# Depthwise convolution: 16 of 31 taps on TensorE as four passes over four stacked, shifted copies of 32 channels, the copies made through memory, and no taps on GpSimd

## The chip, the cores and the metric

The kernel runs on one core of one Trainium2 chip, as one launch. The metric is the device time of that launch in microseconds; of several runs the median counts.

## The reference

Two decoder layers over 256 tokens of width 1024, all in float32. Layer 0 mixes tokens with a causal Conformer convolution, layer 1 with sparse attention; behind each stand a mixture of 32 experts and a gated per-layer embedding. Only the convolution module of layer 0 is touched:

```python
def conv_module(xn, w_pw1, b_pw1, w_dw, b_dw, ln_g, ln_b, w_pw2, b_pw2):
    u = xn @ w_pw1 + b_pw1
    a, g = jnp.split(u, 2, axis=-1)
    u = a * jax.nn.sigmoid(g)
    u = lax.conv_general_dilated(          # depthwise, 31 taps, causal
        u, w_dw[:, None, :].astype(u.dtype), window_strides=(1,),
        padding=[(CONV_WIDTH - 1, 0)], dimension_numbers=("NWC", "WIO", "NWC"),
        feature_group_count=u.shape[-1]) + b_dw
    u = jax.nn.silu(layer_norm(u, ln_g, ln_b))
    return u @ w_pw2 + b_pw2
```

## The kernel before

Each engine has a program of its own, written out by hand, and the programs meet at semaphores. The 1024 channels of the convolution are eight chunks `c` of 128 channels; channels lie on the partitions and the 256 tokens along the free dimension. For one chunk the work goes round the engines:

- TensorE makes both halves of the first pointwise product (L494, `pw1(c)`, 16 matmuls that the trace counts as 32) and signals `pw1_mm`.
- ScalarE takes the sigmoid of the gate half (L1051, `sig_ok`), and then scales the identity by six tap weights into six diagonal matrices (L1057, `dg_ok`).
- VectorE multiplies both halves into the padded row `cv0[:, c]` (L1287, the function `glu`, `glu_ok`). It does this for chunk c+1 only when its own taps of chunk c are through.
- The 31 taps of the chunk are then shared out. VectorE does 20 of them, one instruction each, in two running sums (L1302, L1304, L1306). GpSimd does 5, nine instructions (L955, L958, L959, `ptap_ok`). TensorE does the last 6 as matmuls with the diagonal matrices (L473, the function `taps`, `tap_mm`).
- VectorE adds up the four partial sums (L1316 to L1318, `conv_ok`), and TensorE adds the chunk into the channel sum for the layer norm (L479, `channel_sum`).

TensorE's order is `pw1(c)`, `taps(c-1)`, `channel_sum(c-3)`. From chunk 4 on `pw1(c)` also waits for `glu(c-3)`, since the products share four PSUM banks. Behind the last chunk TensorE does `taps(7)`, the four bias products of the second pointwise layer (L504), the channel sums that are left, and signals `lnmm`; VectorE then starts the layer norm (L1321). The second pointwise product (L518), the router and the 32 experts follow in one chain.

All loads of weights are issued by the SP queue in a fixed order: the four parts of the first pointwise weights (L350), the second (L352), expert 0 (L307, L311). `ple_w_gate` (L357, 4 MB) waits for `pw1(3)`; one block of attention weights (L359) and a third of expert 1 (L307), 4 MB together, wait for `pw1(7)`. The experts' weights go through two slots of a ring (`ring`), and a slot is loaded again when its expert is done. ScalarE issues a few small loads at the very start (L1031) and none later.

Of the kernel before, what the change touches and what calls it, by code (L numbers as in the profile page):

```python
# [65 lines left out]
def build(nc, x, p, positions, g_mix, g_ffn, g_ple, conv_w_pw1, conv_b_pw1, conv_w_dw, conv_b_dw,  # L66
# [3 lines left out]
    with ExitStack() as ctx:  # L70
# [125 lines left out]
        accb = [carve(256) for _ in range(2)]  # L196
        dgb = carve(2 * PE_TAPS * P).rearrange("p (b i q) -> p b i q", b=2, i=PE_TAPS)
        pac = [ppw[:, 2304:2560], ppw[:, 2560:2816]]
        ptm = ppw[:, 2816:3072]
# [661 lines left out]
        def _(pool):  # L861
# [84 lines left out]

            for c in range(KD):
                pool.wait_ge(glu_ok, c + 1)
                if c >= 2:
                    pool.wait_ge(conv_ok, c - 1)  # L950
                for i_ in range(POOL_TAPS):
                    w = TAPS - PE_TAPS - POOL_TAPS + i_
                    u = cv0[:, c, w:w + T]
                    if i_ == 0:
                        g.tensor_scalar(pac[c % 2], u, wdw[:, c, w:w + 1], None, ALU.mult).then_inc(c_pool, 1)  # L955
                        own[0] += 1
                    else:
                        link(g.tensor_scalar(ptm, u, wdw[:, c, w:w + 1], None, ALU.mult))  # L958
                        i = g.tensor_tensor(pac[c % 2], pac[c % 2], ptm, ALU.add)  # L959
                        if i_ < POOL_TAPS - 1:  # L960
                            link(i)
                i.then_inc(ptap_ok, 1)
                pool.wait_ge(ptap_ok, c + 1)
# [748 lines left out]
```

## Time and profile before

| | |
|---|---|
| time, median of 3 runs | 1471.85 us (1470.04 to 1474.88) |
| time of the profiled execution | 1465.78 us |
| span of the profiled execution | 1464.1 us |
| busy: TensorE matmul, VectorE, ScalarE, GpSimd | 1094.6, 344.3, 250.8, 476.2 us |
| moved by DMA | 448.75 MB, 307 GB/s on average |

Busy time is summed over the whole span, whose stages have different limits; the convolution takes the first tenth of it. In the rows of the trace the first number of a timeline is the start in us from the beginning of the span, the second the time taken; PE is TensorE's matmul, PEld its weight load, DVE VectorE, ACT ScalarE, POOL GpSimd, and SPq and ACTq are the times that the queues of SP and ScalarE need to issue a DMA.

### The profile page before, as it was taken

To read this page: it belongs to the slowest core of one execution; us is meant where nothing else is said; L and a number is where in the kernel's file an instruction comes from. 1 tells how busy PE (TensorE), PEld (TensorE's weight loads), DVE (VectorE), ACT (ScalarE), POOL (GpSimd) and SP (SyncE) were. 2 spreads that over 40 slices of the span, in tenths; PEclk is the share of its full clock that TensorE was granted. 3 is DMA by queue.
4 is the path that set the end of the run, shared out by engine and by line. 5 is a ranking of instruction groups with operands and counts; after the bars stand their busy time and mean duration, and the time that the engine had idled before them with its cause. 6 is when DMAs were issued, how large, how long until landed. Compare 5 with 4: busy or idle time off the path is not lost.

```text
span 1464.1 us, 27412 instructions
## 1 busy us (share of the span) xinstructions
PE 1094.6 (75%) x10298; PEld 631.2 (43%) x10299; DVE 344.3 (24%) x958; ACT 250.8 (17%) x598; POOL 476.2 (33%) x799
## 2 busy tenths in 40 slices
PE   5976986766767667677999789876767677677658
PEld 5863553333433333333455554533433334334334
DVE  3997140000000000002417681400000000000011
ACT  3112111110111101111211571111101101011111
POOL 3662043334343343431000130434343343434320
PEclk9996998888888878888999699988888878889879
DMA  8921229999999999998313603599999999998940
GB/s 260 397 103 64 115 74 407 414 413 415 413 414 413 413 415 413 415 413 308 121 56 126 278 2 115 194 414 415 413 415 413 414 414 413 415 412 330 414 179 29
DMA packets 119819, 448.75 MB, mean 307 GB/s; under 512 B 10562, under 2 KB 21442, under 8 KB 103394
## 3 DMA queue, kind: packets, MB, share of 16 engines
q1 hardware_dynamic: 115202, 447.91, 77.0%
q10 hardware_dynamic: 4576, 0.30, 0.2%
q8 instruction: 26, 0.43, 0.1%
q14 instruction: 15, 0.12, 0.0%
HBM read 447.14 MB, written 1.05 MB: 306 GB/s over the span
## 4 chain that ended last, share of the span: by engine, by line
PE 37%; DMA 35%; DVE 6%; issue 4%; PEldq 3%; ACT 2%; PEld 1%; POOL 1%; SPq 1%; POOLq 0%; DVEq 0%
DMA ring<-in_moe_w_up 35%; PE PS L542 13%; PE PS L430 9%; PE PS L557 5%; PE PS L518 2%; PEld PS L564 1%; PEldq L642 1%; PE PS L550 1%; DVE arena L1353 1%; SPq L307 1%; PE PS L729 1%; PE PS L702 1%; ACT arena L1099 1%; PEldq L643 1%; ACT arena L1095 1%
## 5 line engine op out<-in xcount | busy, mean ns | idle before, releaser
L542 PE MATMUL PS<-ring,arena 128*32 128x256 f32 x4128 | 356.2, 516 | 233.9 <-DMA ring<-in_moe_w_up 222.3
L542 PEld LDWEIGHTS PS<-ring,arena 128*32 128x32 f32 x4128 | 170.5, 147 | 410.4 <-issue 252.9
L920 POOL TENSOR_SCALAR arena<-arena 128x32 f32<-128x32 f32 x64 | 18.8, 293 | 538.8 <-PE PS L564 538.8
L1353 DVE TENSOR_TENSOR arena<-PS,arena 64x256 f32<-64x256 f32 x65 | 27.8, 428 | 671.1 <-ACT arena L1095 666.5
L557 PE MATMUL PS<-ring,arena 128*32 128x256 f32 x2080 | 126.0, 381 | 30.8 <-DVE arena L1356 30.8
L1095 ACT ACTIVATE arena<-PS 64x256 f32<-64x256 f32 x64 | 24.2, 378 | 594.7 <-PE PS L542 594.7
L902 POOL TENSOR_SCALAR arena<-arena 128x512 f32<-128x512 f32 x67 | 104.7, 1562 | 3.5 <-DVE arena L1405 3.5
L557 PEld LDWEIGHTS PS<-ring,arena 128*32 128x32 f32 x2080 | 73.4, 109 | 61.1 <-issue 37.5
L895 POOL TENSOR_SCALAR arena<-arena 128x32 f32<-128x32 f32 x268 | 92.5, 366 | 13.6 <-POOL arena L921 13.2
L904 POOL TENSOR_TENSOR arena<-arena 128x512 f32<-128x512 f32 x67 | 85.2, 1272 | 5.6
L564 PE MATMUL PS<-arena 32*128 32x256 f32 x1040 | 74.5, 397 | 9.4 <-ACT arena L1112 0.6
L529 PE MATMUL PS<-hn,arena 128*32 128x256 f32 x1072 | 70.4, 379 | 3.0 <-POOL arena L898 2.1
L430 PE MATMUL PS<-wb,xnT 128*128 128x512 f32 x160 | 71.9, 606 | 0.0
L1348 DVE TENSOR_TENSOR arena<-PS,g 128x256 f32<-128x256 f32 x67 | 28.5, 425 | 170.0 <-PE PS L535 170.0
L889 POOL TENSOR_TENSOR rstd<-rstd,nhalf 128x1 f32<-128x1 f32 x12 | 8.2, 696 | 158.4 <-DVE rstd L1250 158.4
L564 PEld LDWEIGHTS PS<-arena 32*128 32x128 f32 x1040 | 50.3, 183 | 20.2 <-issue 20.2
L1099 ACT COPY arena<-PS 128x256 f32<-128x256 f32 x64 | 23.9, 373 | 168.5 <-PE PS L557 168.5
L906 POOL TENSOR_TENSOR arena<-arena 128x256 f32<-128x256 f32 x67 | 48.8, 728 | 5.3
L1095 ACT ACT_TABLE_LOAD x32 | 41.1, 1283 | 41.2 <-issue 41.1
L430 PEld LDWEIGHTS PS<-wb,xnT 128*128 128x128 f32 x160 | 30.8, 196 | 37.7 <-issue 37.7
L529 PEld LDWEIGHTS PS<-hn,arena 128*32 128x32 f32 x1072 | 33.6, 110 | 27.7 <-POOL arena L898 3.1
L1306 DVE SCALAR_TENSOR_TENSOR arena<-ppw,arena 128x256 f32<-128x256 f32 x72 | 45.1, 626 | 0.0
(309 smaller groups left out, 1271.0 us busy)
## 6 DMA issues: line engine op xcount, KB each, us to landing
ring<-in_moe_w_up SPq DMA_DIRECT2D x64, 2048.0 KB, 17.5
ring<-in_moe_w_down SPq DMA_DIRECT2D x64, 2048.0 KB, 22.1
ring<-in_moe_w_gate SPq DMA_DIRECT2D x63, 2048.0 KB, 12.9
wb<-in_ple_w_gate SPq DMA_DIRECT2D x4, 2048.0 KB, 20.6
ring<-in_conv_w_pw SPq DMA_DIRECT2D x3, 2048.0 KB, 19.3
ring<-in_nsa_w_in SPq DMA_DIRECT2D x3, 2048.0 KB, 18.2
wb<-in_nsa_w_in SPq DMA_DIRECT2D x2, 2048.0 KB, 9.0
wb<-in_nsa_cmp_w SPq DMA_DIRECT2D x2, 2048.0 KB, 8.4
```

The lines of the kernel that those rows point to most:

```text
L430: i = pe.matmul(PS[:, bank, :], lhs[:, k, t * P:(t + 1) * P], w[:, k, :], start=start and k == 0, stop=(k == KD - 1))
L529: i = pe.matmul(PS[32 * j:32 * j + 32, BGX, 0:Q4], lhs[:, t, :], hn[:, t, Q4 * j:Q4 * (j + 1)], start=(t == 0), stop=(t == NT - 1))
L542: i = pe.matmul(PS[32 * j:32 * j + 32, BGU, 0:256], xT[:, k, :], w[:, k, 256 * (j % 2):256 * (j % 2 + 1)], start=(k == 0), stop=(k == 7))
L557: i = pe.matmul(PS[32 * j:32 * j + 32, BY, 0:Q4], hT[:, c, 32 * f:32 * f + 32], w_dn(s)[:, f, c, Q4 * j:Q4 * (j + 1)], start=(q == 0), sto ...
L564: i = pe.matmul(PS[:, ACC + j, 256 * t:256 * (t + 1)], w[32 * j:32 * j + 32, t * P:(t + 1) * P], ysb[32 * j:32 * j + 32, :], start=False, ...
L895: i = g.tensor_scalar(eq4[:, t, k, :], c32, S4[:, t, k:k + 1], None, ALU.is_equal)
L902: g.tensor_scalar(eqr, srow, cc, None, ALU.is_equal).then_inc(count, 1)
L904: g.tensor_tensor(eqr, eqr, wrow, ALU.mult).then_inc(count, 1)
L906: g.tensor_tensor(to_wT, eqr[:, 0, :], eqr[:, 1, :], ALU.add).then_inc(w_ok, 1)
L1095: nc.scalar.activation(gs[64:128, :], PS[0:64, BGU, 0:256], ACT.Silu).then_inc(sil_ok, 1)
L1306: i = v.scalar_tensor_tensor(out=o, in0=u, scalar=wdw[:, c, w:w + 1], in1=o, op0=ALU.mult, op1=ALU.add)
L1353: return v.tensor_tensor(hh[64:128, :], PS[64:128, BGU, 0:256], gs[64:128, :], ALU.mult)
```

## The change

TensorE does 16 taps in place of 6, GpSimd none in place of 5, and VectorE 15 in place of 20. To put 16 taps into few matmuls, the 128 rows of the array are used as four taps of 32 channels each: an operand `xst` holds, for a group `q` of 32 channels, four copies of the row, each shifted by one token more, one on each quarter of the partitions. Sixteen matmuls of 128 rows and 32 columns (four passes `m` for each of four groups `q`) then do 16 taps of 128 channels. Their weights `dgb` are built by GpSimd in one instruction a chunk, from a 0/1 pattern `stk` and the tap weights `wst`.

[...] ScalarE's queue writes the row of the chunk to memory (`xdram`, 128 rows of 1084 bytes), waits until it is there, and reads it back in four DMAs, one for each shift (each 32 partitions x 4 groups, pieces of 1072 bytes). The tap weights take the same way once, ahead of the first sigmoid, in rows of 512 bytes and pieces of 128 bytes. Line numbers of the changed kernel are 9 higher from SP's program on, 10 in GpSimd's.

```diff
-PE_TAPS, POOL_TAPS = 6, 5
+PE_TAPS, STACK = 16, 4
+RUNS = PE_TAPS // STACK
+DVE_TAPS = TAPS - PE_TAPS
+XW = T + STACK * (RUNS - 1)
...
             def taps(c):
-                pe.wait_ge(glu_ok, c + 1)
                 pe.wait_ge(dg_ok, c + 1)
                 if c >= 2:
                     pe.wait_ge(conv_ok, c - 1)
-                for i_ in range(PE_TAPS):
-                    w = TAPS - PE_TAPS + i_
-                    i = pe.matmul(PS[:, 4 + c % 2, 0:T], dgb[:, c % 2, i_, :], cv0[:, c, w:w + T],
-                                  start=(i_ == 0), stop=(i_ == PE_TAPS - 1))
+                pe.wait_ge(xst_in[c % 2], 16 * STACK * (c // 2 + 1))
+                for m in range(RUNS):
+                    for q in range(4):
+                        i = pe.matmul(PS[32 * q:32 * q + 32, 4 + c % 2, 0:T], dgb[c % 2][:, q, m, :],
+                                      xst[c % 2][:, q, STACK * m:STACK * m + T], start=(m == 0), stop=(m == RUNS - 1))
                 i.then_inc(tap_mm, 1)
...
+            link(g.tensor_scalar(stk[:, :], iot[:, :], colp[:, 0:1], None, ALU.is_equal))
+            pool.wait_ge(wst_in, 16 * (1 + STACK))
             for c in range(KD):
-                pool.wait_ge(glu_ok, c + 1)
                 if c >= 2:
-                    pool.wait_ge(conv_ok, c - 1)
-                for i_ in range(POOL_TAPS):
...
+                    pool.wait_ge(tap_mm, c - 1)
+                shape = [P, 4, RUNS, 32]
+                g.tensor_tensor(dgb[c % 2], stk[:, :].unsqueeze(1).unsqueeze(1).broadcast_to(shape),
+                                wst[:, :, c, :].unsqueeze(3).broadcast_to(shape), ALU.mult).then_inc(dg_ok, 1)
...
             norm(0, ROW_MIX)
+            act.wait_ge(vec_ok, 4)
+            act.dma_start(wdram, wch.rearrange("p j c m -> p (j c m)")).then_inc(wst_in, 16)
+            act.wait_ge(wst_in, 16)
+            for j in range(STACK):
+                act.dma_start(wst[32 * j:32 * j + 32, :, :, :].rearrange("p q c m -> p q (c m)"),
+                              wdram.rearrange("(q p) (j n) -> j p q n", q=4, j=STACK)[j]).then_inc(wst_in, 16)
             for c in range(KD):
...
                 if c >= 2:
                     act.wait_ge(tap_mm, c - 1)
-                for i_ in range(PE_TAPS):
-                    w = TAPS - PE_TAPS + i_
-                    i = nc.scalar.activation(dgb[:, c % 2, i_, :], ident[:, :], ACT.Copy, scale=wdw[:, c, w:w + 1])
-                i.then_inc(dg_ok, 1)
+                act.wait_ge(glu_ok, c + 1)
+                act.dma_start(xdram[c], cv0[:, c, DVE_TAPS:]).then_inc(xst_out, 16)
+                act.wait_ge(xst_out, 16 * (c + 1))
+                for j in range(STACK):
+                    act.dma_start(xst[c % 2][32 * j:32 * j + 32, :, :],
+                                  xdram[c].rearrange("(q c) u -> c q u", q=4)[:, :, j:j + XW]).then_inc(xst_in[c % 2], 16)
...
-                nv = TAPS - PE_TAPS - POOL_TAPS
-                for w in range(nv):
-                    o = cT[:, c, :] if w % 2 == 0 else accb[0]
+                for w in range(DVE_TAPS):
+                    o = cT[:, c, :] if w % 2 == 0 else accb
...
                 dve.wait_ge(c_dve, own[0])
+                link(v.tensor_tensor(cT[:, c, :], cT[:, c, :], accb, ALU.add))
                 dve.wait_ge(tap_mm, c + 1)
-                dve.wait_ge(ptap_ok, c + 1)
-                link(v.tensor_tensor(accb[1], PS[:, 4 + c % 2, 0:T], pac[c % 2], ALU.add))
-                link(v.tensor_tensor(cT[:, c, :], cT[:, c, :], accb[0], ALU.add))
-                v.tensor_tensor(cT[:, c, :], cT[:, c, :], accb[1], ALU.add).then_inc(conv_ok, 1)
+                v.tensor_tensor(cT[:, c, :], PS[:, 4 + c % 2, 0:T], cT[:, c, :], ALU.add).then_inc(conv_ok, 1)
```

How this stands in ScalarE's program, from the copies of the normed input (L1017) over chunks 0 and 1 to chunk 2, before the change:

```order
L1017 ACTIVATE xnT<-PS,vecT 128x128 x3
L1051 ACT_TABLE_LOAD
L1051 ACTIVATE arena<-PS,vecT 128x256 [waits pw1_mm]
L1057 ACTIVATE arena<-ident,arena 128x128 x6
L1051 ACTIVATE arena<-PS,vecT 128x256 [waits pw1_mm]
```

and in the changed kernel, the same place, as far as the sigmoid of chunk 1 (`tap_rows` and `glu_rows` are the tensors in memory):

```order
L1018 ACTIVATE xnT<-PS,vecT 128x128 x3
L1049 DMA tap_rows<-arena 128x128 [waits vec_ok]
L1052 DMA arena<-tap_rows 32x4x32 [waits wst_in]
L1052 DMA arena<-tap_rows 32x4x32 x3
L1058 ACT_TABLE_LOAD
L1058 ACTIVATE arena<-PS,vecT 128x256 [waits pw1_mm]
L1063 DMA glu_rows<-ppw 128x271 [waits glu_ok]
L1066 DMA ppw<-glu_rows 32x4x268 [waits xst_out]
L1066 DMA ppw<-glu_rows 32x4x268 x3
L1058 ACTIVATE arena<-PS,vecT 128x256 [waits pw1_mm]
```

The six scalings have gone, and five DMAs a chunk have come, with a wait between the first and the others; the next sigmoid stands behind them in the same queue.

TensorE's program at the end of the convolution, from the last pointwise product to the layer norm's second sum, before the change:

```order
L494 MATMUL PS<-xnT,ring 128x256 [waits xt_act] x4
L473 MATMUL PS<-ppw,arena 128x256 [waits conv_ok,dg_ok,glu_ok]
L473 MATMUL PS<-ppw,arena 128x256 x5
L479 MATMUL PS<-hn,ones 128x256 [waits conv_ok]
L473 MATMUL PS<-ppw,arena 128x256 [waits conv_ok,dg_ok,glu_ok]
L473 MATMUL PS<-ppw,arena 128x256 x5
L504 MATMUL PS<-arena,ones 128x512 x4
L479 MATMUL PS<-hn,ones 128x256 [waits conv_ok] x3
L509 MATMUL PS<-xnT,ones 128x256 [waits ln_sq] x8
```

and in the changed kernel:

```order
L503 MATMUL PS<-xnT,ring 128x256 [waits xt_act] x4
L482 MATMUL PS<-ppw 32x256 [waits xst_in0,conv_ok,dg_ok]
L482 MATMUL PS<-ppw 32x256 x15
L488 MATMUL PS<-hn,ones 128x256 [waits conv_ok]
L482 MATMUL PS<-arena 32x256 [waits xst_in1,conv_ok,dg_ok]
L482 MATMUL PS<-arena 32x256 x15
L513 MATMUL PS<-arena,ones 128x512 x4
L488 MATMUL PS<-hn,ones 128x256 [waits conv_ok] x3
L518 MATMUL PS<-xnT,ones 128x256 [waits ln_sq] x8
```

The order of the pieces is the same; the taps are 16 matmuls in place of 6, and their wait is now for the copies (`xst_in`) and no longer for the row itself (`glu_ok`).

## Rows read from the trace of the kernel before

**Rows 1.** The page: DMA share in 40 slices of the span, and the chain's shares.

```profile
DMA  8921229999999999998313603599999999998940
PE 37%; DMA 35%; DVE 6%; issue 4%; PEldq 3%; ACT 2%; PEld 1%; POOL 1%; SPq 1%; POOLq 0%; DVEq 0%
```

**Rows 2.** Timeline of chunk 6, VectorE and TensorE; brackets: idle before, releaser.

```profile
89.43 0.47 DVE L1287 SCALAR_TENSOR_TENSOR ppw<-PS,vecT,arena 128x256 f32<-128x256 f32 x1
...
99.11 0.47 DVE L1306 SCALAR_TENSOR_TENSOR arena<-ppw,arena 128x256 f32<-128x256 f32 x1
99.51 0.47 DVE L1306 SCALAR_TENSOR_TENSOR hn<-ppw,arena,hn 128x256 f32<-128x256 f32 x1
...
101.89 0.47 DVE L1287 SCALAR_TENSOR_TENSOR ppw<-PS,vecT,arena 128x256 f32<-128x256 f32 x1
...
102.41 4.54 PE L473 MATMUL PS<-ppw,arena 128*128 128x256 f32 x12 [2.26 <-DVE ppw L1287]
```

**Rows 3.** Timeline of the first chunks, TensorE, ScalarE and VectorE.

```profile
27.97 0.47 ACT L1051 ACTIVATE arena<-PS,vecT 128x256 f32<-128x256 f32 x1 [5.29 <-PE PS L494]
...
34.68 2.75 PE L473 MATMUL PS<-ppw,arena 128*128 128x256 f32 x12
...
37.27 7.07 PE L494 MATMUL PS<-xnT,wb 128*128 128x256 f32 x32
...
56.27 0.59 PE L479 MATMUL PS<-hn,ones 128*128 128x256 f32 x2
```

**Rows 4.** Timeline of the end of the convolution, TensorE and VectorE.

```profile
114.86 5.49 PE L473 MATMUL PS<-ppw,arena 128*128 128x256 f32 x12 [7.47 <-DVE ppw L1287]
120.28 3.82 PE L504 MATMUL PS<-arena,ones 1*128 1x512 f32 x8
124.02 2.08 PE L479 MATMUL PS<-hn,ones 128*128 128x256 f32 x4
...
127.87 0.42 DVE L1318 TENSOR_TENSOR hn<-hn,arena 128x256 f32<-128x256 f32 x1
129.68 0.42 DVE L1321 TENSOR_SCALAR arena<-PS 128x256 f32<-128x256 f32 x1 [1.38 <-PE PS L479]
```

**Rows 5.** The chain that ended last, one piece of the experts' stage.

```profile
206.23 1.97 PE PS L557 x32
```

**Rows 6.** The page's groups: a two-input GpSimd instruction of 512 elements.

```profile
L904 POOL TENSOR_TENSOR arena<-arena 128x512 f32<-128x512 f32 x67 | 85.2, 1272 | 5.6
```

**Rows 7.** DMA issues: count, KB each, median us to landing.

```profile
ring<-in_conv_w_pw SPq DMA_DIRECT2D x3, 2048.0 KB, 19.3
...
ppw<-in_p SPq DMA_DIRECT2D x1, 256.0 KB, 2.7
...
out_h<-h SPq DMA_DIRECT2D x1, 512.0 KB, 2.6
```

**Rows 8.** SP's DMA queue from 34 to 36 and 50 to 54 us: packets, MB, share.

```profile
q1 hardware_dynamic: 370, 0.76, 101.8%
...
q1 hardware_dynamic: 410, 1.64, 102.6%
```

**Rows 9.** Timeline: issues of DMAs by SP and ScalarE.

```profile
7.13 1.79 ACTq L1031 DMA_DIRECT2D posi<-in_positions  x1
...
25.34 9.96 SPq L352 DMA_DIRECT2D ring<-in_conv_w_pw  x2
...
43.66 2.66 SPq L311 DMA_DIRECT2D ring<-in_moe_w_down  x1
...
53.87 7.14 SPq L357 DMA_DIRECT2D wb<-in_ple_w_gate  x2
...
100.60 0.58 SPq L307 DMA_DIRECT2D ring<-in_moe_w_gate  x1
```

**Rows 10.** Stretches of two us: length, busy by engine, granted clock, DMA.

```profile
104.00:106.00 2.00, 2.00 (x6) 1.56 (x5) 2.00 (x4) 0.00 (x0) 1.82 (x3) 0.50 1.05 406
...
118.00:120.00 2.00, 2.00 (x6) 1.35 (x4) 2.00 (x5) 0.00 (x0) 1.82 (x3) 0.50 0.00 0
```

More of the change, by code:

```diff
@@ L77, in build @@
         PS = ctx.enter_context(nc.psum_tensor("PS", [P, 8, 512], F32))
+        xdram = nc.dram_tensor("glu_rows", (KD, P, T + STACK * RUNS - 1), F32, kind="Internal").ap()
+        wdram = nc.dram_tensor("tap_rows", (P, STACK * 8 * RUNS), F32, kind="Internal").ap()
         ring = sb("ring", [P, 2, 12288])
@@ L98, in build @@
         colp = sb("colp", [P, 1])
+        stk = sb("stk", [P, 32])
         xtot = sb("xtot", [P, 1])
@@ L195, in build @@
         wdw = carve(8 * TAPS).rearrange("p (c w) -> p c w", c=8)
[L196 to L199, printed above, removed]
+        accb = carve(256)
+        wch = carve(STACK * 8 * RUNS).rearrange("p (j c m) -> p j c m", j=STACK, c=8)
+        wst = carve(8 * 4 * RUNS).rearrange("p (q c m) -> p q c m", q=4, c=8)
+        xst = [x_.rearrange("p (q u) -> p q u", q=4) for x_ in (ppw[:, 2304:2304 + 4 * XW], carve(4 * XW))]
+        dgb = [x_.rearrange("p (q m s) -> p q m s", q=4, m=RUNS) for x_ in (ppw[:, 3392:3392 + 512], carve(512))]
         bpw2 = carve(1024)[0:1, :]
@@ L252, in build @@
         att_in, gate_in, mask_ok, c_bld = sem("att_in"), sem("gate_in"), sem("mask_ok"), sem("c_bld")
-        tap_mm, dg_ok, ptap_ok, root_in, root_ok = sem("tap_mm"), sem("dg_ok"), sem("ptap_ok"), sem("root_in"), sem("root_ok")
+        tap_mm, dg_ok, wst_in, root_in, root_ok = sem("tap_mm"), sem("dg_ok"), sem("wst_in"), sem("root_in"), sem("root_ok")
+        xst_in, xst_out = [sem(f"xst_in{i}") for i in range(2)], sem("xst_out")
         x_bld = sem("x_bld")
@@ L884, in _ @@
                 link(g.iota(ioti[32 * q:32 * q + 32, 0:1], pattern=[[0, 1]], base=0, channel_multiplier=1))
-            g.tensor_copy(colp[:, :], ioti[:, 0:1]).then_inc(const_ok, 1)
+            link(g.tensor_copy(colp[:, :], ioti[:, 0:1]))
+            g.memset(mcol[:, 6:7], 0.0).then_inc(const_ok, 1)
             def rsqrt(n, x):
@@ L945, in _ @@
             rsqrt(2, rstd[:, 1, 1:2])
+            link(g.tensor_scalar(stk[:, :], iot[:, :], colp[:, 0:1], None, ALU.is_equal))
+            pool.wait_ge(wst_in, 16 * (1 + STACK))
             for c in range(KD):
-                pool.wait_ge(glu_ok, c + 1)
                 if c >= 2:
-                    pool.wait_ge(conv_ok, c - 1)
-                for i_ in range(POOL_TAPS):
[L952 to L963, printed above, removed]
+                    pool.wait_ge(tap_mm, c - 1)
+                shape = [P, 4, RUNS, 32]
+                g.tensor_tensor(dgb[c % 2], stk[:, :].unsqueeze(1).unsqueeze(1).broadcast_to(shape),
+                                wst[:, :, c, :].unsqueeze(3).broadcast_to(shape), ALU.mult).then_inc(dg_ok, 1)
             rsqrt(3, rstd[:, 1, 0:1])
@@ L1276, in first_columns @@
                 dve.wait_ge(vtr, 3)
-                v.tensor_copy(wdw, PS[:, 2, 0:8 * TAPS].rearrange("p (c w) -> p c w", c=8)).then_inc(vec_ok, 1)
-                dve.wait_ge(vec_ok, 3)
+                taps = PS[:, 2, 0:8 * TAPS].rearrange("p (c w) -> p c w", c=8)
+                v.tensor_copy(wdw, taps).then_inc(vec_ok, 1)
+                v.tensor_copy(wch, taps[:, :, DVE_TAPS:].rearrange("p c (m j) -> p j c m", j=STACK)).then_inc(vec_ok, 1)
+                dve.wait_ge(vec_ok, 4)
                 link(v.memset(cv0[:, :, 0:TAPS - 1], 0.0))
```

## The prediction

> **What bounds the kernel now.** I read the page first: its chain of waits gives TensorE 37% and DMA 35%, and the DMA share over the span shows where, at 9 in the two experts' stages and 1 or 2 in the third to the sixth slice [rows 1]. The change lies in the first 130 us, so the question is whether the end of the convolution passes on to the end of the kernel. It does: the experts' weights are loaded when a slot of the ring comes free, so that stage starts as late as its first expert, and nothing with a time of its own stands between. I therefore count the moment at which VectorE starts the layer norm, 129.7 us [rows 4], and carry its shift to the end one for one.
>
> Within the convolution I read the timeline. One chunk takes 101.89 - 89.43 = 12.5 us, and VectorE has no gap in it: it is the bound [rows 2]. Its taps run 0.40 us apart where GpSimd is silent [rows 2]; 20 of them with the product for the next chunk (0.4) and three additions (1.4) make 9.8 us, and the other 2.7 are what GpSimd's taps cost VectorE. TensorE needs 7.1 us for the pointwise product, 2.75 for six taps, 0.6 for a sum, 10.4 in all, and waits 2 us or more in each late chunk [rows 2, 3]. Behind the last chunk TensorE's taps, the bias products and two sums are done by 126.1, before VectorE's last addition at 127.9 to 128.3; after that only one sum is left, 1.4 us to the layer norm [rows 4].
>
> **What the change takes away.** VectorE: 15 taps (6.1 us), the product (0.4) and two additions (0.9) are 7.4 us a chunk. GpSimd's one instruction of 512 elements takes 1.3 [rows 6] and can hold VectorE up by no more than that: 8.7 at worst. ScalarE's six scalings are off. TensorE: 16 matmuls of 32 columns are 32 instructions in the trace's count, and 32 such took 1.97 us in the experts [rows 5], less than the 2.75 of now. So TensorE becomes the bound at 7.1 + 2.0 + 0.6 = 9.7 us a chunk, unless the copies are late.
>
> **What the bounce costs with a quiet DMA.** The trace has no such bounce; the nearest rows bound it. A write of 512 KB to memory lands 2.6 us after issue, a read of 256 KB 2.7 us [rows 7]. At the 0.4 MB/us that the engines move [rows 8], the write of 139 KB is 0.9 shorter: 1.8. Four reads of 137 KB leave about 0.4 us apart, so the last lands 1.3 + 2.7 = 4.0 after the first issue. Together 5.8 us from the gated row to the copies, below the 9.7 of a chunk: quiet, it is hidden in all chunks but the last. The Trainium skill (SBUF — State Buffer, "The DMA setup-cost knee") speaks against the change here: about 2 us fixed per transfer whatever its size, which by an estimate from its fit is 2.3 for the write where the row gives 1.8. By the page the three exposed bounces would cost 1.5 us more than in the sum below.
>
> **What it costs with a busy DMA.** From the start to about 75 us SP's loads keep all engines full [rows 1, 8]. Pieces of 2 KB took 370 in 2 us x 16 engines, 88 ns each; pieces of 4 KB 410 in 4 us, 160 ns [rows 8]. The write gives each engine 8 pieces, the reads 32. If ScalarE's pieces and SP's alternate, the write gains 0.7 and the reads 2.8 us beside 2 KB pieces (9.3 in all), 1.3 and 5.1 beside 4 KB (12.2). Lower bound nothing (5.8), if a small queue is served at once.
>
> A second cost is the issue. SP's own queue is held 5 us for one DMA of 2 MB (9.96 for two, 7.14 for two later), and ScalarE once 1.8 us for a load of 0.5 KB while SP was also issuing [rows 9]. If the descriptors of both queues come from one place, a DMA of ScalarE can stand up to 5 us behind one of SP's, twice in a bounce: between 0 and 10 us. I take 1.3 a side, half of the mean of that wait, for chunks 0, 1 and 3, which fall beside SP's held issues (until 46 us, and when `ple_w_gate` is issued behind `pw1(3)`) [rows 9]. When SP issues behind `pw1(7)` it is not held (0.58 us) [rows 9]; there I take 1 in all.
>
> **The sum**, as times of the new kernel:
> - `pw1(1)` ends at 34.7, as now [rows 3]. The tap weights' own bounce stands ahead of the first sigmoid, which starts at 27.97 now after 5.3 us of idle. Those 5.3 us hide a quiet bounce up to its last issue; beside SP's loads I take 1.5 us more than they hide (0 to 4), so the row of chunk 0 is gated at 30.5.
> - Chunk 0: 5.8 + 3.5 + 2.6 = 11.9, copies at 42.4. TensorE, which now starts its taps at 34.7, waits 7.7 us. Two chunks of taps and product (9.1 each) bring `pw1(3)` to 60.6; chunk 1's copies (ScalarE is through with chunk 0's reads at 37.3, VectorE with its taps at 36.6; gated at 38.2, there at 50.1) are in time.
> - Chunk 2: product ready at 51.5, gated 1.1 later, 12.2 beside 4 KB pieces: 64.8. TensorE waits 4.2 us.
> - Four chunks of 9.7 end `pw1(7)` at 103.6. Chunk 3 (11.9) is in time; chunk 4, still beside SP's backlog since ScalarE adds 0.69 MB a chunk, is 0.7 late: 104.3. Now it ends at about 100, where SP's next DMAs leave [rows 9].
> - Chunk 7: gated at 105.4. SP has just issued 4 MB behind the same product, 2 KB and then 4 KB pieces: 5.8 + 0.7 + 4.0 + 1.0 = 11.5, copies at 116.9.
> - What is queued behind those copies on TensorE now stands in the path: taps (2.0 at full clock; 3.9, which I take, at half after such a wait), bias products 3.8, three sums (0.6 each, 1.0 at the lower clock) 2.2 [rows 3, 4]. The layer norm can start at 126.8, against 129.7: 2.9 us gained.
> - The clock. After its idle 2.3 us the 12 tap instructions at 102.4 took 4.5 us and after 7.5 us 5.5, not 2.75, with a granted clock of 0.50, the 1.2 GHz level, in the stretches there [rows 2, 4, 10]. The waits of 7.7 and 4.2 us can each bring that: 0 to 5.4 us in all, of which I take 1.8, what the short wait cost.
>
> Left is a gain of 1.1 us. The profiled execution of now, 1465.78 in all, would be one of about 1464.7; it lies 6.1 below the median of the runs, so for the median 1471.85 - 1.1 = 1470.7 us. In short: VectorE's 40 us (8 x 5) are saved, and TensorE, the bounces and the tail eat them.
>
> **The rivals.** A measurement of this kernel tells about 0.3%, 4.4 us, from no change.
> - *Forecast: it cancels out, within 4.4 us of now.* Chance 0.36; its own range 1467 to 1476.
> - *Faster: ScalarE's DMAs are served past SP's.* For it: its loads at the start were issued in 0.4 to 1.8 us with SP's queue full. With 5.8 us for chunks 0 to 6 TensorE never waits after chunk 0; chunk 0 is there at 36, `pw1(7)` ends at 93, and with 10.5 for chunk 7 and 10 for the tail the layer norm starts at 114: 15.5 gained, 1456. With the pieces alternating but no held issue it is 5 to 6 us, 1466. Chance 0.33 for both. Against it: the queue was full and a load took 19.3 us to land [rows 7].
> - *Slower: ScalarE's DMAs stand behind SP's in issue.* Place: chunks 0, 1 and 3 while SP is held. Each us more a side costs about 2 us for chunk 0 and, when chunk 1 or 3 is late too, 1 to 2 more. At 4 us a side chunk 0's copies come at 50, chunk 3's 5 late, and `pw1(7)` ends past 115: 12 us lost, 1484. It decides from about 2.5 us a side on, where the loss passes 4.4. Chance 0.27.
> - *Slower by another way: VectorE stays the bound.* From its cycle of 8.7 at worst against 9.7 I give this 0.04.
>
> **The numbers.** Faster by over 0.3%: 0.33; within: 0.36; slower: 0.31. The range leaves out the best of the fast case and the worst of the slow one: 1457 to 1484.
>
> **What would show it.** In the changed kernel's trace: VectorE's taps 0.40 apart, and gaps in VectorE that were not there. Taps on TensorE of 2 us at full clock. Idle of TensorE before the taps of chunks 0, 2 and 7, released by the read DMAs: 8, 4 and 10 us; none before 1, 5 and 6. ScalarE's issues: write to first read 1.8 us late in the stage, over 3 early. `pw1(7)` at 104, the layer norm 10 us behind the last copies. I am wrong if reads issued before 60 us land within 5 us (faster), or if ScalarE's queue is held for several us at one issue (slower); or if the shift at the layer norm is not the shift at the end.

## The result, and the profile after

The changed kernel takes 1487.22 us (median of 4 runs, 1480.12 to 1490.93) against 1471.4 (4 runs): ratio 1.0098, 95% interval 1.0056 to 1.0141. It is slower, and the forecast of no measurable change (1470.7, range 1457 to 1484) was wrong. The profiled execution takes 1480.12 us with a span of 1478.4, 14.3 more than before; the layer norm starts at 145.16, 15.5 later than in [rows 4]. So the shift does pass on to the end, and what is lost is lost in the convolution.

The page of the changed kernel: DMA share in 40 slices, and the chain's shares by engine and by line; the copies and the write (`glu_rows`) are in it with 2% each.

```profile
DMA  8955028999999999999303801589999999999950
PE 41%; DMA 40%; DVE 6%; issue 4%; ACT 3%; PEldq 2%; PEld 1%; SPq 1%; POOL 1%; ACTq 0%; POOLq 0%; DVEq 0%
DMA ring<-in_moe_w_up 35%; PE PS L551 13%; PE PS L439 9%; PE PS L566 5%; PE PS L527 2%; DMA arena<-glu_rows 2%; PE PS L503 2%; DMA glu_rows<-ppw 2%; PEld PS L573 1%; PEldq L651 1%; PE PS L559 1%; DVE arena L1361 1%; SPq L316 1%; PE PS L738 1%; PE PS L711 1%
```

Its waits of TensorE from 18 to 150 us (in all, times, the longest):

```profile
PE PS L482 <- DMA arena<-glu_rows: 18.9, 3, 14.1
PE PS L482 <- DMA ppw<-glu_rows: 18.4, 2, 12.3
```

And its timeline, cut to the DMAs of ScalarE for chunks 0, 4 and 7 (L1063 the write, L1066 the reads), TensorE's taps (L482), and what stands behind the last copies:

```profile
30.12 0.34 ACTq L1063 DMA_DIRECT2D glu_rows<-ppw  x1
35.99 1.76 ACTq L1066 DMA_DIRECT2D ppw<-glu_rows  x4
46.28 3.64 PE L482 MATMUL PS<-ppw 128*32 128x256 f32 x32 [12.28 <-DMA ppw<-glu_rows]
60.56 3.47 PE L482 MATMUL PS<-arena 128*32 128x256 f32 x32 [3.44 <-DMA arena<-glu_rows]
77.29 3.64 PE L482 MATMUL PS<-ppw 128*32 128x256 f32 x32 [6.16 <-DMA ppw<-glu_rows]
89.64 0.34 ACTq L1063 DMA_DIRECT2D glu_rows<-ppw  x1
89.82 1.93 PE L482 MATMUL PS<-arena 128*32 128x256 f32 x32 [1.36 <-DMA arena<-glu_rows]
91.60 1.76 ACTq L1066 DMA_DIRECT2D ppw<-glu_rows  x4
108.62 1.93 PE L482 MATMUL PS<-arena 128*32 128x256 f32 x32
118.02 1.94 PE L482 MATMUL PS<-ppw 128*32 128x256 f32 x32
119.27 0.34 ACTq L1063 DMA_DIRECT2D glu_rows<-ppw  x1
125.58 1.76 ACTq L1066 DMA_DIRECT2D arena<-glu_rows  x4
134.72 3.64 PE L482 MATMUL PS<-arena 128*32 128x256 f32 x32 [14.14 <-DMA arena<-glu_rows]
138.29 3.94 PE L513 MATMUL PS<-arena,ones 1*128 1x512 f32 x8
145.16 0.42 DVE L1329 TENSOR_SCALAR arena<-PS 128x256 f32<-128x256 f32 x1 [6.25 <-PE PS L488]
```

The reader is to see three things. Where the engines of the DMA are quiet (chunks 4 to 6) the change does what it says: 118.02 - 108.62 = 9.4 us a chunk against 12.5 in [rows 2], and no wait. Where SP's loads are under way (0 to 3, and 7) TensorE waits for the copies, 37.4 us in all. And each long wait is followed by taps of 3.64 us in place of 1.93, at a granted clock of 0.50 (the 1.2 GHz level) in place of 1.00 (2.4 GHz), as a stretch behind the longest wait and one in the quiet chunks show (columns as in [rows 10]):

```profile
134.80:138.00 3.20, 3.20 (x32) 1.46 (x32) 0.00 (x0) 0.00 (x0) 0.00 (x0) 0.50 0.00 0
93.00:99.00 6.00, 6.00 (x30) 5.19 (x28) 5.46 (x15) 0.00 (x0) 0.00 (x0) 1.00 0.33 83
```

The DMA issues of the changed kernel, first from 89 to 94 us (quiet), then from 20 to 90; then what the two queues moved in the first microsecond of the quiet write, and in the first 3.6 us of chunk 7's (q1 is SP's queue, q10 ScalarE's):

```profile
ppw<-glu_rows ACTq DMA_DIRECT2D x4, 134.0 KB, 3.0
glu_rows<-ppw ACTq DMA_DIRECT2D x1, 135.5 KB, 1.9
...
ppw<-glu_rows ACTq DMA_DIRECT2D x8, 134.0 KB, 8.0
...
glu_rows<-ppw ACTq DMA_DIRECT2D x5, 135.5 KB, 6.3
...
q10 hardware_dynamic: 61, 0.07, 18.4%
...
q1 hardware_dynamic: 556, 1.14, 92.7%
```

The last answer has no line for q10: between 119.3 and 122.9 not one piece of the write had been moved, while SP's queue moved 556. SP had issued its two DMAs at 118.12 and 118.53, in less than 1 us; nothing was held in issue.

| bounce of chunk | gated row to copies, predicted | measured | of it the write leg |
|---|---|---|---|
| 0 | 11.9 | 16.2 | 5.9 |
| 1 | 11.9 | 21.7 | 8.7 |
| 2 | 12.2 | 19.0 | 6.3 |
| 3 | 11.9 | 17.5 | 6.7 |
| 4 | 9.3 (5.8 if quiet) | 6.3 (it was quiet) | 2.0 |
| 7 | 11.5 | 15.4 | 6.3 |

(Chunk 4: the last of the reads is issued 1.3 us after 91.60 and lands 3.0 later.)

The rest of a bounce can be seen in the same way. What the queues moved from 36.0 to 39.4 us (behind the issue of chunk 0's reads at 35.99), from 64.6 to 68.0 (behind chunk 2's at 64.62), from 40 to 44, and from 39.2 to 46.9:

```profile
q1 hardware_dynamic: 659, 1.32, 105.3%
...
q1 hardware_dynamic: 239, 1.47, 104.9%
...
q1 hardware_dynamic: 402, 0.82, 71.9%
q10 hardware_dynamic: 407, 0.39, 35.6%
...
q1 hardware_dynamic: 908, 1.83, 75.6%
q10 hardware_dynamic: 720, 0.69, 31.5%
```

The first two have no line for q10 either. On all six legs on which ScalarE's queue was empty before (the reads of chunks 0 to 3, the write and the reads of chunk 7) the first piece came 3.4 to 3.7 us after the first issue; in the quiet it came after 0.9. From then on the two queues take turns, one piece each (402 to 407). And the last answer explains the longest bounce. The write of chunk 1, issued at 38.89, stood in ScalarE's own queue behind chunk 0's reads: the 720 pieces are those of the four reads and of the write, in one run (512 and 128 rows, and 16 more pieces for each of the five DMAs).

### The profile page after: what moved, and what is told of

It is laid out like the page before. It is cut to its first block, busy times and chain, and to the rows that moved or that the text cites. A ratio compares the mean times of both kernels' runs of the same rounds, so it can differ in the third digit from the quotient of the medians.

```text
span 1478.4 us, 27619 instructions
## 1 busy us (share of the span) xinstructions
PE 1090.7 (74%) x10458; PEld 621.4 (42%) x10459; DVE 303.9 (21%) x911; ACT 236.5 (16%) x550; POOL 423.2 (29%) x737
## 4 chain that ended last, share of the span: by engine, by line
PE 41%; DMA 40%; DVE 6%; issue 4%; ACT 3%; PEldq 2%; PEld 1%; SPq 1%; POOL 1%; ACTq 0%; POOLq 0%; DVEq 0%
DMA ring<-in_moe_w_up 35%; PE PS L551 13%; PE PS L439 9%; PE PS L566 5%; PE PS L527 2%; DMA arena<-glu_rows 2%; PE PS L503 2%; DMA glu_rows<-ppw 2%; PEld PS L573 1%; PEldq L651 1%; PE PS L559 1%; DVE arena L1361 1%; SPq L316 1%; PE PS L738 1%; PE PS L711 1%
## 5 line engine op out<-in xcount | busy, mean ns | idle before, releaser
L566 PEld LDWEIGHTS PS<-ring,arena 128*32 128x32 f32 x2080 | 73.0, 109 | 61.3 <-issue 37.4
L503 PE MATMUL PS<-xnT,wb 128*128 128x256 f32 x192 | 43.0, 381 | 0.2 <-DVE xnT L1267 0.2
```

The source lines that it names most:

```text
L503: i = pe.matmul(PS[:, c % 4, g * T:(g + 1) * T], w[:, k, (c % 4) * P:(c % 4 + 1) * P], xnT[:, k, :], start=(k == 0), stop=(k == KD - 1))
L566: i = pe.matmul(PS[32 * j:32 * j + 32, BY, 0:Q4], hT[:, c, 32 * f:32 * f + 32], w_dn(s)[:, f, c, Q4 * j:Q4 * (j + 1)], start=(q == 0), sto ...
```

## The experiments

Theory: a small DMA of ScalarE waits behind the pieces of SP's loads that already lie at the 16 engines, once for each leg, and its pieces then take turns with SP's. Rivals: the bounce is dear by itself; the number or size of its pieces is what costs; or the loss is not the copies'. All ratios are to the kernel before, timed beside each; runs of different groups are compared by these ratios and by the layer norm's start, since the spans of single executions of one kernel differ by about 10 us. The two measures go together: in all twelve kernels the shift of the layer norm and the shift of the time by the ratio agree to about 5 us.

| run | median, us | ratio, 95% interval | layer norm starts |
|---|---|---|---|
| changed kernel | 1487.22 | 1.0098 (1.0056 to 1.0141) | 145.16 |
| a1_hold_last | 1478.82 | 1.0059 (1.0038 to 1.0079) | 135.47 |
| a2_hold_all | 1457.16 | 0.9935 (0.9913 to 0.9956) | 118.99 |
| a3_before_hold | 1469.30 | 1.0017 (0.9998 to 1.0036) | 128.43 |
| a4_pieces | 1492.09 | 1.0155 (1.0119 to 1.0192) | 155.59 |
| b1_direct | 1488.72 | 1.0137 (1.0107 to 1.0166) | 153.78 |
| b2_rows16 | 1484.37 | 1.0092 (1.0063 to 1.0121) | 148.28 |
| b3_hold_fill | 1454.96 | 0.9908 (0.9874 to 0.9941) | 113.93 |
| b4_diag8 | 1451.69 | 0.9875 (0.9847 to 0.9903) | 113.14 |
| c1_hybrid | 1447.37 | 0.9864 (0.9837 to 0.9890) | 107.30 |
| c2_diag6 | 1458.39 | 0.9928 (0.9909 to 0.9948) | 119.47 |
| c3_diag7 | 1453.37 | 0.9903 (0.9883 to 0.9922) | 115.25 |

### SP's loads out of the way

**a1_hold_last.**

```diff
-            sp.wait_ge(pw1_mm, 8)
+            sp.wait_ge(xst_in[1], 16 * STACK * (KD // 2))
             sp.dma_start(dense(WB[2]), cols(nsa_w_in[0], 2)).then_inc(in_in[2], 16)
```

> SP's 4 MB behind the last pointwise product are issued when the copies of chunk 7 have landed, not before; nothing else differs from the changed kernel. Backlog theory (a small DMA of ScalarE waits behind SP's pieces that already lie at the 16 engines): chunk 7's bounce falls from 15.4 us (write issued 119.27, taps 134.72) to the 5 or 6 of the quiet chunks, TensorE's idle before those taps from 14.1 to 5 us, and the kernel is 9 to 10 us faster than the changed one, near 1477 us. Rival (a bounce at the end is slow by itself, because nothing else hides the way to memory and back, or because TensorE's clock is low behind a wait): the bounce stays at 14 to 16 us and the time within 0.3% of 1487.

Measured: the layer norm starts 9.7 us earlier than in the changed kernel, as expected; by the ratios 0.4% or 5.7 us are left of it at the end, with intervals that overlap. In its timeline chunk 7's taps wait 5.23 us where they waited 14.14:

```profile
125.03 3.54 PE L482 MATMUL PS<-arena 128*32 128x256 f32 x32 [5.23 <-DMA arena<-glu_rows]
```

The bounce at the same place is 6.5 us long (write issued at 118.48) and not 15.4. It is not dear by itself, and the low clock is not what makes it long: the taps behind it still take 3.54 us.

**a2_hold_all.** SP's loads behind the first pointwise weights wait for the same semaphore, and the embeddings' loads come ahead of expert 0's.

```diff
+            sp.wait_ge(xst_in[1], 16 * STACK * (KD // 2))
             for n in range(2):
                 sp.dma_start(dense(PW2[n]), cols(conv_w_pw2[0], n)).then_inc(w2_in[n], 16)
+            sp.wait_ge(conv_ok, KD)
+            embeddings(0)
             expert(0, 0, 0)
```

> All of SP's loads behind the 8 MB of first pointwise weights wait until chunk 7's copies have landed, so only chunk 0 is near SP's traffic; the loads of the embeddings now stand before expert 0's. Backlog theory: every bounce 5 to 6 us, TensorE idle before its taps only in chunk 0 (2 to 5 us) and chunk 7 (5), the last pointwise product ends at 93 to 96 us (118.1 in the changed kernel), the layer norm starts at 110 to 114 (145.2), 31 to 35 us faster than the changed kernel, 1452 to 1456 us, which is also faster than the kernel before by 1%. Rival 1 (the bounce's cost is its own, not SP's backlog): no more than 10 us faster than the changed kernel. Rival 2 (the convolution does get short, but the delayed loads give it back in the experts' stage): the layer norm starts at 112 and the end of the span moves by less than half of that.

Measured: the layer norm starts 26.2 us earlier, by the ratios the time is 1.6% or 24 us less than that of the changed kernel, and 0.65% less than before. The layer norm at 118.99 is 5 us behind what was expected (110 to 114). Its timeline keeps two waits for copies:

```profile
43.12 3.64 PE L483 MATMUL PS<-ppw 128*32 128x256 f32 x32 [8.89 <-DMA ppw<-glu_rows]
...
108.55 3.64 PE L483 MATMUL PS<-arena 128*32 128x256 f32 x32 [5.12 <-DMA arena<-glu_rows]
```

The first is longer than expected (8.9, not 2 to 5): the first pointwise weights themselves keep the engines full until about 41 us, so chunk 0's bounce (write issued at 31.79) still lies beside them. Little is given back later (26.2 us at the layer norm, 24 in the time): the rival of late loads falls.

**a3_before_hold**, the control: the same order of loads in the kernel before, held until `glu_ok` 8.

> The kernel before with the same loads of SP held back until its last product of the gate (glu 7), a control: if SP's traffic beside the convolution costs anything by itself (clock, memory ports, VectorE), this one is faster than the kernel before as well. Backlog theory: within 0.3% of the kernel before, 1467 to 1476 us, since no engine of the kernel before waits for a small DMA there. Rival: faster by 5 us or more, and then that part of what the kernel with all loads held back gains is not the bounces'.

Measured: the same time as before (its interval contains 1), though the second pointwise weights leave at 113.6 us and not at 25.3. So what a2 wins is the bounces', not some other benefit of quiet engines.

### The legs and the pieces

**a4_pieces.**

```diff
-                act.dma_start(xdram[c], cv0[:, c, DVE_TAPS:]).then_inc(xst_out, 16)
+                act.dma_start(xdram[c].rearrange("s (q u) -> q s u", q=4), cv0[:, c, DVE_TAPS:]).then_inc(xst_out, 16)
...
-                                  xdram[c].rearrange("(q c) u -> c q u", q=4)[:, :, j:j + XW]).then_inc(xst_in[c % 2], 16)
+                                  xdram[c][:, j:j + 3 * XD + XW]).then_inc(xst_in[c % 2], 16)
```

> The rows are laid out in memory so that each partition's four rows lie in one stretch: the four reads have 128 pieces of 4.3 KB in place of 512 of 1.07 KB, the write is as it was, SP's loads are where they were. Backlog theory with pieces that take turns (an engine does one piece of ScalarE's, one of SP's): from the first read's issue to the last landing the busy chunks take 7 to 9 us in place of 9 to 13 (the wait for the first piece, 3.5 to 4 us, stays), TensorE's idle of 12.3, 3.4, 6.2 and 14.1 us before taps 0, 1, 2 and 7 falls by 2 to 4 us each, and the kernel is 8 to 12 us faster than the changed one, near 1477. Rival (bytes take turns, or the whole leg is waiting time before the first piece): idle times as in the changed kernel, time within 0.3% of 1487.

Measured: not faster; the layer norm starts 10.4 us later, and the ratio is 1.0155 for 1.0098. The reads did what was expected: from the first issue to the taps 8.1, 9.2, 9.9 and 6.1 us in chunks 0, 1, 2 and 7, in place of 10.3, 12.9, 12.7 and 9.1. The write, which I had taken to be as it was, did not: 8.8, 9.8, 13.9 and 10.4 us in place of 5.9, 8.7, 6.3 and 6.3. Its timeline for chunk 2, and the DMA share from 97 to 107 us (40 slices; the write stands left, the reads right):

```profile
59.90 0.53 ACTq L1064 DMA_DIRECT2D glu_rows<-ppw  x1
73.77 0.31 ACTq L1067 DMA_DIRECT2D ppw<-glu_rows  x1
...
DMA  0000022222520000008796979971000000000000
```

A share of 0.2 is about four engines of 16: the write's outermost dimension is now the four groups. The Trainium skill (DMA: Bandwidth & Descriptors, "Why a DMA increments its semaphore by 16 and not by 1") says that the number of engines is the largest one up to 16 that divides the outermost dimension of both sides, here 4 and 128; this trace agrees. The mishap is a good measurement. Each of the four engines has 32 pieces, not 8, and the write leg grows from 2.0 to 3.6 us in the quiet and, in chunk 2, from 6.3 to 13.9 beside SP's loads: 24 more pieces cost 0.07 us each quiet, 0.32 there, where SP's pieces are 4 KB and more, and 0.12 in chunk 0 beside pieces of 2 KB. From 64 to 68 us the queues moved:

```profile
q1 hardware_dynamic: 278, 1.61, 97.5%
q10 hardware_dynamic: 76, 0.08, 5.7%
```

If SP's 278 are spread evenly over the 16 engines, 70 of them are on these four, beside ScalarE's 76: one for one, as in the changed kernel (402 to 407 on all 16). Pieces take turns, as the prediction had it.

Not all of the 10.4 us is the copies'. They come 7.1 us later; the other 3.3 are the bias products behind the taps, which took 3.94 us in the changed kernel and here

```profile
145.43 7.19 PE L514 MATMUL PS<-arena,ones 1*128 1x512 f32 x8
145.50:152.50 7.00, 7.00 (x8) 2.42 (x8) 0.42 (x1) 0.00 (x0) 0.00 (x0) 0.50 0.52 187
```

at a granted clock of 0.50, where the changed kernel had 0.95 from 138.4 to 142.2 us. b1 and b2 show the same 7.19, so their layer norms too are 3.3 us later than their copies make them. Why the clock came back there in the changed kernel, a1 and a2, and not in these three, no run shows.

**b2_rows16.** The same layout, the write as four DMAs of 32 rows.

```diff
+                for q in range(4):
+                    act.dma_start(xdram[c][:, XD * q:XD * q + XD], cv0[32 * q:32 * q + 32, c, DVE_TAPS:]).then_inc(xst_out, 16)
```

> The layout in memory of the run with reads of 4.3 KB, but the write is four DMAs of 32 rows each. In that run the write alone took 13.9 us beside SP's loads (6.3 in the changed kernel) and 3.6 quiet (2.0), with a DMA share near 0.25, as if only four of the 16 engines took part with 32 pieces each; its reads took 2 to 3 us less. If a quarter of the engines was its cost, this write takes 7 to 8.5 us busy (6.3 and 1.3 for the three further issues), the reads stay 2 to 3 us shorter, and the time comes 2 to 6 us under the changed kernel: 1481 to 1485. Rival (the layout of the rows in memory made the write slow): the write stays at 12 to 14 us and the time at 1492.

Measured: the write leg of chunks 0, 1, 2 and 7 is back at 6.2 to 7.2 us (chunk 3's took 9.7), so a quarter of the engines was its cost. The reads' median landing between 20 and 90 us is 6.7 to 6.8, not 8.0: a quarter of the pieces save 1.3 us, half of what I expected. The copies of chunk 7 come at 134.55, as in the changed kernel (134.72); that the layer norm is 3.1 us later is the slow bias products. The ratio is that of the changed kernel (1.0092 and 1.0098). The number of pieces is the smaller part of a leg.

**b1_direct.** Sixteen DMAs from row to copy, one for each shift and group, without memory between.

```diff
-                act.dma_start(xdram[c], cv0[:, c, DVE_TAPS:]).then_inc(xst_out, 16)
-                act.wait_ge(xst_out, 16 * (c + 1))
...
+                    for q in range(4):
+                        act.dma_start(xst[c % 2][32 * j:32 * j + 32, q, :],
+                                      cv0[32 * q:32 * q + 32, c, DVE_TAPS + j:DVE_TAPS + j + XW]).then_inc(xst_in[c % 2], 16)
```

> No way through memory for the rows: 16 DMAs a chunk (32 partitions each) copy straight from the row to the four shifted places, with no write and no wait between; SP's loads as in the changed kernel. Backlog theory (each leg of the bounce waits for its own first piece, 3.5 to 4 us beside SP's backlog against 1 us with quiet engines): only one such wait is left, but 16 issues cost ScalarE about 7 us; from the gated row to the copies 9 to 12 us in the busy chunks in place of 15 to 22, TensorE's idle before taps 0, 2 and 7 about 4 to 5 us less each, 8 to 14 us faster than the changed kernel, 1473 to 1479. With quiet engines it is slower than the bounce, 8 to 9 us against 5. Rival (what is slow is the number of small pieces beside SP's, and 16 DMAs of 32 rows have as many pieces as the four reads had): the leg takes as long as the reads did behind the issues, 14 us or more, and the time is within 0.3% of the changed kernel.

Measured: no gain. The 16 issues take ScalarE 10.2 us and not 7, more than a chunk of TensorE, so now the quiet chunks wait too. From the gated row to the copies it takes 15.4, 17.9 and 14.3 us in chunks 0, 2 and 7, where the theory had 9 to 12 and the rival 14 or more: by its number the rival was nearer. The parts say otherwise: in chunk 0 the last of the 16 leaves 9.6 us after the first and lands 5.8 later. And b1 gives the cleanest look at the cause: DMAs of 33.5 KB, two pieces for each engine, first from 30 to 45 us beside SP's loads, then from 90 to 105 in the quiet (median us to landing):

```profile
ppw<-ppw ACTq DMA_DIRECT2D x16, 33.5 KB, 5.6
arena<-ppw ACTq DMA_DIRECT2D x5, 33.5 KB, 5.4
...
ppw<-ppw ACTq DMA_DIRECT2D x15, 33.5 KB, 1.9
```

3.5 to 3.7 us more for two pieces an engine. Turns with SP's pieces of 2 KB (88 ns in [rows 8]) would explain 0.2 of them. The rest, some 3.4, is waiting that two pieces cannot explain. On the bounce's legs 2.5 to 2.8 of it are seen directly, as the later first piece (3.4 to 3.7 us for 0.9), and each leg pays it.

### What else fills the wait, and the split without copies

**b3_hold_fill.** a2 with two channel sums and the bias products ahead of `taps(7)`.

```diff
-            taps(KD - 1)
+            for c in range(KD - 3, KD - 1):
+                channel_sum(c)
+            pe.wait_ge(glu_ok, KD)
             for n in range(2):
...
+            taps(KD - 1)
```

> The kernel with all of SP's later loads held back, and on TensorE the two channel sums and the four bias products that stood behind taps 7 now stand before them, in the wait for chunk 7's copies. The copies come as before at 108.5 us; behind them are left taps (3.6), one sum and VectorE's addition. Theory (TensorE waits 5.1 us there for nothing): the layer norm starts 5 us earlier, near 114, and the kernel takes 1452 us, 5 less than the one it is built on. Rival (the clock: taps behind a busy stretch at full clock win 1.7 us more): 1450. Rival (the end of the convolution no longer sets the second pointwise product, its weights come late): no gain, 1457.

Measured: the layer norm starts at 113.93, 5.1 us earlier, as expected. In the time less of it is seen: a ratio 0.3% lower than that of a2, with intervals that overlap. The taps, now behind a busy stretch at full clock, took 3.22 us at a granted clock of 0.58, so the rival that had them at full clock fell.

**b4_diag8, c2_diag6, c3_diag7.** The kernel before, without copies and without GpSimd's taps: 8, 6 or 7 taps on TensorE as diagonals, the rest on VectorE.

```diff
-PE_TAPS, POOL_TAPS = 6, 5
+PE_TAPS, POOL_TAPS = 8, 0
```

> The kernel before with another split and no copies: TensorE 8 taps with 128 x 128 diagonals in place of 6, GpSimd none, VectorE 23 in place of 20; SP's loads as before. From the rows of the kernel before: TensorE 7.1 + 8 x 0.46 + 0.6 = 11.4 us a chunk, VectorE 23 x 0.40 + 0.4 + 0.9 = 10.5 when GpSimd is silent, against 12.5 now. Theory (part of what the change wins is only that GpSimd's taps are gone, which cost VectorE 2.7 us a chunk): about 1 us a chunk, the layer norm at 121 to 124, 6 to 9 us faster than the kernel before, near 1462. Rival (VectorE's 2.7 us a chunk were not GpSimd's doing): VectorE's taps come more than 0.5 us apart here too, 12.5 us a chunk or more, and the time is that of before or longer.

> The kernel before with GpSimd's five taps given to VectorE (TensorE 6, VectorE 25), nothing else: one part of the change alone. VectorE's chunk is then 25 x 0.40 + 0.4 + 0.9 = 11.3 us, against the 12.5 that 20 taps take beside GpSimd. Theory (GpSimd's taps cost VectorE more time than the five taps they take off it): 1 to 1.3 us a chunk less, the layer norm at 118 to 121, 8 to 11 us faster than the kernel before. Rival (GpSimd's help is worth something, and the eight-tap kernel gained by TensorE's two more taps alone): time of the kernel before or above.

> The same with seven taps on TensorE and 24 on VectorE. With eight, TensorE has no gap (10.8 us a chunk) and VectorE waits 0.6 us for it; with seven TensorE needs 10.35 and VectorE 10.7 to 10.9. Expected: 10.8 to 10.9 a chunk and the time of the eight-tap kernel within 0.3%, 1450 to 1455; the two are the same optimum. Rival (TensorE's busy time, not VectorE's, sets every chunk): 3 us faster.

Measured: c2, where VectorE does 25 taps in place of 20 and GpSimd none (which also spares VectorE one addition), is 0.72% faster than before. Its last additions of two chunks stand 11.0 us apart, with more work than the 12.5 of [rows 2]:

```profile
84.86 0.42 DVE L1297 TENSOR_TENSOR hn<-PS,hn 128x256 f32<-128x256 f32 x1
...
95.86 0.42 DVE L1297 TENSOR_TENSOR hn<-PS,hn 128x256 f32<-128x256 f32 x1
```

GpSimd's five taps cost VectorE more than they took off it. Where it happens stands in the timeline of the kernel before, in chunk 6:

```profile
94.02 0.73 POOL L959 TENSOR_TENSOR ppw<-ppw 128x256 f32<-128x256 f32 x1
94.08 0.95 DVE L1306 SCALAR_TENSOR_TENSOR arena<-ppw,arena 128x256 f32<-128x256 f32 x1
94.85 0.97 POOL L958 TENSOR_SCALAR ppw<-ppw,arena 128x256 f32<-128x256 f32 x1
94.95 0.69 DVE L1306 SCALAR_TENSOR_TENSOR hn<-ppw,arena,hn 128x256 f32<-128x256 f32 x1
```

Taps that take 0.47 us alone take 0.95 and 0.69 here. The taps of 94.95, 95.57 and 95.97 are followed by one at 96.84: three take 1.9 us where they would take 1.2 alone, and four such rounds make the 2.7 us a chunk. The Trainium skill (SBUF — State Buffer, "Terms") says that the two engines share one pair of ports, held for a whole instruction, and that the loser is blocked. The trace agrees that VectorE is held up, but not for the whole of GpSimd's instruction: the tap of 94.95 ends at 95.64, before the instruction of 94.85 does (95.82; times of GpSimd are rough).

b4 is 1.25% faster than before, 18 us, where 6 to 9 were expected. With 8 taps TensorE has no gap between 33.7 and 111.4 us, and the layer norm comes at 113.14, far ahead of my 121 to 124: I had put the gain at 1 us a chunk, where it is 12.5 - 10.8 = 1.7; and `glu(7)`, for which TensorE waits 7.5 us in [rows 4], comes in time. c3 is as fast as b4 within the intervals, as expected.

**c1_hybrid.** Chunks 0 and 1 with eight diagonals, 2 to 7 with copies, SP's loads held, and the filling of b3.

```diff
+                if c < ND:
...
+                    for i_ in range(DIAG):
+                        w = TAPS - DIAG + i_
+                        i = pe.matmul(PS[:, 4 + c % 2, 0:T], dia[c][:, i_, :], cv0[:, c, w:w + T],
+                                      start=(i_ == 0), stop=(i_ == DIAG - 1))
```

> Chunks 0 and 1 do eight taps with 128 x 128 diagonals and no copies (VectorE 23 there), chunks 2 to 7 the changed kernel's 16 taps from copies; SP's later loads wait for the last copies, and sums and bias products fill TensorE's wait for them. So no bounce lies beside SP's backlog and the first one is due only after the last product of chunk 3. Backlog theory: no idle of TensorE before taps 0 to 6, last pointwise product at 92 to 94 us, copies of chunk 7 at 99 to 100, layer norm at 104 to 106 where the eight-tap kernel without copies has it at 113 to 114; 7 to 9 us faster than that one: 1443 to 1445. Rival (the bounces of chunks 2 and 3 are still late behind the last pointwise weights): layer norm at 110 or later, no faster than 1450.

Its only wait for copies, in the waits of TensorE from 18 to 120 us:

```profile
PE PS L493 <- DMA ppw<-glu_rows: 0.9, 1, 0.9
```

Measured: 1447.37, 2 us above what was expected, the layer norm at 107.30, 1 to 3 later. Chunk 7's taps start at 101.71 right behind the bias products, without a wait, and still take 3.64 us:

```profile
101.80:105.30 3.50, 3.50 (x32) 1.29 (x32) 0.82 (x2) 0.00 (x0) 0.00 (x0) 0.50 0.77 241
```

The clock was down before them: 0.79 over the bias products (one row of the array each, 97.3 to 101.7 us). Idle time is not the only thing that it falls behind. It is the fastest median of all, but its interval and that of b4 overlap, and the two were not timed against each other; b4 needs no copies and leaves SP's order as it was.

## Why the prediction was wrong

Right: that the convolution decides, and that its shift is the shift at the end (15.5 at the layer norm, 14.3 in the span, 15.8 between the medians). TensorE's bound: 9.4 us a chunk for 9.7. VectorE's taps 0.40 apart. In the quiet a write of 2.0 for 1.8, and no wait in chunks 5 and 6. The quiet bounce in all: 6.3 for 5.8. The issue: ScalarE's four reads take 1.8 to 2.1 us to issue whether SP is busy or not, so the rival of a queue held in issue fell; that its time, 1484, was the nearest is luck. The turns of the pieces, one for one (402 to 407; a4: 76 to 70), and nearly their size: chunk 0's reads took 6.0 us more than chunk 4's, 2.8 of them before the first piece, 3.2 after it, where the prediction had 2.8 for turns.

The step that failed is the size of the busy bounce: 5.8 quiet, 0.7 to 1.3 and 2.8 to 5.1 for turns, and for held issues 2.6 in chunks 0, 1 and 3, 1.0 in chunk 7 and nothing in chunk 2; 11.5 to 12.2 in all. Measured 15.4 to 21.7. The sum let the turns begin at once. They begin only when a DMA's first piece has come up, and beside SP's loads that is 2.5 to 2.8 us later than in the quiet, once for the write and once for the reads (at 119.3 no piece in 3.6 us, at 89.7 already 61 in the first one; b1 lands 3.5 to 3.7 later). The 1.3 a side that I took for held issues stood, by another cause, for a wait twice as long, and it was set at 0.5 a side in chunk 7 because SP's issue there is short; the backlog is 4 MB all the same.

The Trainium skill (DMA: Bandwidth & Descriptors, "Queues, rings and completion order") says that an engine drains a whole packet, typically 9 to 17 descriptors, of one queue before it turns to the next. By an estimate from that page, 17 of SP's pieces would be 1.4 us at 36 us, where they took 0.08 each, and 3.9 at 65, where they took 0.23. The trace does not agree: the start was 2.8 and 2.5 us later than in the quiet, 41 and 15 of SP's pieces went by on each engine, and afterwards the turns were one for one.

A second step failed in chunk 1: the sum had its copies at 50.1, in time, and they came at 60.6, since its write waited in ScalarE's own queue for chunk 0's late reads (8.7 us for the leg). TensorE waited 3.4 us where the prediction had none.

The balance, by the sum's own terms: `pw1(7)` ends at 118.1 and not 104.3. TensorE's waits up to there were 23.2 us for 12.6 in the sum (10.6 more); its taps at the lower clock took 5 us more, where the sum had set 1.8 apart, behind everything; a chunk of 9.4 for 9.7 and `pw1(1)` 0.7 earlier give 2 back. Chunk 7's bounce is 4 longer, its tail 10.4 for 9.9. Together 18.4, from 126.8 to 145.2; less the 1.8 that the sum had set apart, this is the way from 1.1 us gained to 15.5 lost.

Two slips in the working are small. 2.6 less 0.9 is 1.7 for the quiet write, not 1.8. And the 1.5 us by which the Trainium skill's fit (SBUF — State Buffer, "The DMA setup-cost knee") was to make it worse counts the write alone: by an estimate from the same fit a read is 2.3 us where the row gave 2.7, so a bounce is 5.9 for 5.8. Measured quiet were 1.9 to 2.0 for the write and 3.0 for a read.

The range failed with the term: the "4 us a side" of the rival held only in issue and only in chunks 0, 1 and 3, so no case had chunks 2 and 7 late by it as well.

What stays open: what sets the 3.4 to 3.7 us before the first piece (it was the same behind 41 pieces of SP's an engine and behind 15; 1.2 to 1.5 MB went by); and why reads with the same large pieces were 2.2 to 3.7 us shorter in a4 and 0.5 to 2.0 in b2. Nor did any run make the shifted copies with an engine in place of a DMA, so whether the stacked taps need the bounce at all was not tried.

## What to carry to other kernels

Before a small DMA is put on the critical path, look at what the 16 engines have before them then, on whatever queue: beside a stream of large loads each dependent leg waited 2.5 to 2.8 us longer for its first piece, and took turns after that. If it must be there, hold back the loads that are not yet needed; here the first of them could wait from 25 to 114 us without a measurable cost (a3), and the same change went from 1% slower to 0.7% faster. And try the simple part alone first: taking GpSimd's taps away was worth 0.7% by itself, two more diagonals on TensorE 0.5% beyond, without one DMA.

## What the runs showed of the hardware

- A DMA of 33.5 KB from ScalarE's queue lands in 1.9 us on quiet engines and in 5.4 to 5.6 beside SP's stream.
- The first piece of a DMA from ScalarE's queue moved 0.9 us after its issue on quiet engines, and 3.4 to 3.7 us after it beside SP's stream, whether 41 or 15 of SP's pieces passed on each engine meanwhile. After that the two queues moved piece for piece (402 to 407 in 4 us).
- A DMA issued behind others of its own queue waited for their pieces too: chunk 1's write leg took 8.7 us behind chunk 0's reads.
- A DMA whose outermost dimension is 4 ran on about a quarter of the engines: share 0.2, and the write leg grew from 2.0 to 3.6 us in the quiet and from 6.3 to 13.9 in chunk 2.
- TensorE's taps took 3.2 to 3.6 us in place of 1.93 behind waits of 3.4 us and more, and also behind bias products without any wait (c1, granted clock 0.50).
- Sixteen issues of small DMAs took ScalarE 10.2 us, 0.64 each; four with 128 or more pieces took 1.76, 0.44 each.
- Five taps on GpSimd lengthened VectorE's chunk of 20 taps to more than its chunk of 25 without them (12.5 and 11.0 us).
